# A chunked recurrence whose products are split into a part without the state and a part with it

## The chip, the cores and the metric

One core of one Trainium2 chip runs the whole program. The metric is device time in microseconds (us). The kernel before takes 5064.52 us, the median of three runs (5061.65 to 5067.53).

## The reference

The program is three transformer-like blocks, one after the other, on 1024 tokens of 1024 features in float32. The change lies in the third. That block projects its input, runs a latent attention of 4 heads (`mla_attention`) and beside it a recurrence over tokens for 8 heads of 64 channels, and joins both with a gate and an output projection. The recurrence keeps a 64x64 state S per head:

```python
def step(S, inp):
    r_t, w_t, k_t, v_t, kk_t, a_t = inp
    sa = jnp.einsum('bhvk,bhk->bhv', S, -kk_t)
    S = (S * w_t[:, :, None, :] + sa[..., None] * (kk_t * a_t)[:, :, None, :]
         + v_t[..., None] * k_t[:, :, None, :])
    return S, jnp.einsum('bhvk,bhk->bhv', S, r_t)

xs = tuple(jnp.moveaxis(t.astype(jnp.float32), 1, 0) for t in (r, w, k, v, kk, a))
_, ys = lax.scan(step, jnp.zeros((B, H, N, N), jnp.float32), xs)
```

The outputs `ys` are normalised per head, a bonus term is added, and the result is gated and projected.

## The kernel before

Everything is held with features on partitions, x as `xT`, a tile of 128 partitions by 8 by 1024 that stays in SBUF through the whole program. Work is cut into phases. A phase allocates tiles and semaphores, gives each engine its instructions in a fixed, unrolled order written by hand, and ends when all are done; the next begins then. All transfers named below but a few go over the queue of SyncE (SP); ScalarE (ACT) issues some stores. A queue is worked in order, and so is each engine.

The recurrence is computed in 16 chunks (`NCH`) of 64 tokens (`N = CHUNK`). The 8 heads lie as 4 pairs (`NP`), a pair on 128 partitions; a "block" tile holds a pair as two 64x64 blocks on the diagonal of 128x128, so that one product does both heads. From the decays, `recurrence_inputs_phase` makes four arrays of 512 x 1024: alpha (the key of the past, kk, scaled), beta, kappa and rho (the receptance r, scaled), and stores each row block of 128 to DRAM over ScalarE's queue (L3564). `recurrence_phase` ("wkv" in the trace) then does, per chunk:

- scores of beta against alpha and rho (L3756, eight passes for four pairs), a mask on VectorE (L3825) that gives the system N, stored to DRAM (L3661), and a masked copy for later over ScalarE and GpSimd (L3853, L3729);
- scores of kappa against alpha and rho, copied by ScalarE (L3858) and masked by GpSimd (L3734, L3738). These run beside the back substitution.

After the 16th system is stored, all are loaded back at once, twice 2 MB, with one of the 128 (chunk, head) systems per partition (L3704), and VectorE inverts them by back substitution: 62 steps of an outer product (L3835) and an addition (L3838), each waiting for the one before. The inverse is stored (L3710) and read back as blocks (L3687). Then comes the loop over chunks, in which every product waits for the state or for loads made after the output of the chunk before last (L3653, L3657): beta, kappa and v are transposed on TensorE (L3779) and copied by ScalarE (L3866); the right side w is kappa's mask times v plus alpha times the state; u is the inverse times -w (L3841 copies it); the growth is kappa times v plus beta times u; VectorE adds the state (L3843) and scales by the chunk's decay `ends` (L3845); the output y is three products in one bank, copied (L3879) and stored (L3881). All products of the loop are in float32 and have line L3747.

Ahead of it, `latent_attend_phase` ("mla") puts its 16 output stores (L827) on SyncE's queue behind the loads of all four heads (L816 to L822); VectorE copies outputs to two tiles in turn (L983) and waits for the store before last. Behind it, `last_phase` loads weights and the two halves of the tokens (L3935, L3940, L3947, L3952), multiplies, and adds x, which it transposes from `xT` (L4035).

Of the kernel before, what the change touches and what calls it, by code (L numbers as in the profile page):

```python
# [14 lines left out]
P = 128  # L15
# [754 lines left out]
def latent_attend_phase(nc, name, ident, causal, n_heads, q_rows, qr_rows, k_rows, kr_rows, v_rows, out_rows, scale):  # L770
# [15 lines left out]
    with Phase(nc, name) as ph:  # L786
# [20 lines left out]
        stored = [ph.sem(f"stored{b}") for b in range(2)]  # L807
        block = ph.block()

        @block.sync  # L810
        def _(sp):
# [19 lines left out]
            for hd in range(n_heads):  # L831
                load(hd)
            for m in range(NU // 2):
                store(m)
            for b in range(2):
                sp.wait_ge(stored[b], 16 * (NU // 4))

# [2641 lines left out]
def recurrence_inputs_phase(nc, name, block_ones, ps_rows, kk, decay_sig, rate, k_a, r_k, ends, bonus, out):  # L3479
# [6 lines left out]
    with Phase(nc, name) as ph:  # L3486
# [5 lines left out]
        outs = [ph.sb(f"out{n}", [P, T]) for n in range(4)]  # L3492
# [19 lines left out]
        def _(dve):  # L3512
# [12 lines left out]
            for c in range(RC):  # L3525
# [13 lines left out]
                if c:  # L3539
                    dve.wait_ge(stored, 64 * c)  # L3540
                link(tt(outs[0][:, :], p_prev[:, :], kk[:, c, :], ALU.mult))
                link(tt(outs[1][:, :], rate[:, c, :], kk[:, c, :], ALU.mult))
                link(tt(outs[1][:, :], outs[1][:, :], p_inv[:, :], ALU.mult))
                link(tt(outs[2][:, :], kf[:, :], p_inv[:, :], ALU.mult))
                link(tt(outs[3][:, :], p_now[:, :], r[s][:, :], ALU.mult))
# [9 lines left out]
        def _(act):  # L3555
            for c in range(RC):
# [6 lines left out]
                for n in range(4):  # L3563
                    act.dma_start(out[n][c * P:(c + 1) * P, :], outs[n][:, :]).then_inc(stored, 16)  # L3564
            act.wait_ge(stored, 64 * RC)
# [22 lines left out]
def recurrence_phase(nc, name, ident, masks_dram, ends, alpha_d, beta_d, kappa_d, rho_d, v_d, y_dram, system_d, inverse_d):  # L3588

# [7 lines left out]
    BANKS = 4  # L3603
    with Phase(nc, name) as ph:
        masks = ph.sb("masks", [P, 2, P])
        moving = [ph.sb(f"alpha_rho{s}", [P, NP, 2, N]) for s in range(2)]
        be_sb, ka_sb, v_sb, al_sb = ([ph.sb(f"{n}{s}", [P, NP, P]) for s in range(2)] for n in ("be", "ka", "v", "al"))
        bt_all, rk_all = ph.sb("bt_all", [P, NCH, NP, P]), ph.sb("rk_all", [P, NCH, NP, N])
        rb_all = ph.sb("rb_all", [P, NCH, NP, N])
        n_sb = [ph.sb(f"n{s}", [P, NP, N]) for s in range(2)]  # L3610
        rb_raw, kr_raw = ([ph.sb(f"rb_raw{s}", [P, NP, N]) for s in range(2)], [ph.sb(f"kr_raw{s}", [P, NP, 2, N]) for s in range(2)])
        shared = ph.sb("shared", [P, 2 * N * N + 1024])
        system = shared[:, 0:N * N].rearrange("p (j i) -> p j i", i=N)
        inverse_flat = shared[:, N * N:2 * N * N]
        inverse = inverse_flat.rearrange("p (j i) -> p j i", i=N)
        outer = shared[:, 2 * N * N:]
        part = lambda n: shared[:, n * NP * P:(n + 1) * NP * P].rearrange("p (q n) -> p q n", n=P)
        xt_sb = [part(s) for s in range(2)]
        beta_tok, kappa_tok, v_tok = ([part(2 + 2 * n + s) for s in range(2)] for n in range(3))
        w_sb, u_sb, state, grown = (ph.sb(n, [P, NP, P]) for n in ("w", "u", "state", "grown"))  # L3620
        y_sb = [ph.sb(f"y{s}", [P, NP, N]) for s in range(2)]
        score_ps = [ph.ps(f"score{b}", [P, NP, 2, N]) for b in range(BANKS)]
        tok_ps = [ph.ps(f"tok{b}", [P, NP, P]) for b in range(2)]
# [25 lines left out]
        def _(sp):  # L3649
# [41 lines left out]
            for c in range(NCH):  # L3691
                if c >= 2:
                    sp.wait_ge(n_scored, c - 1)
# [842 lines left out]
```

## Time and profile before

| | |
|---|---|
| median of three runs | 5064.52 us |
| profiled execution | 5060.78 us |
| its span | 5059.0 us |
| TensorE matmul busy | 4028.3 us, 80% |
| VectorE busy | 2727.6 us, 54% |
| ScalarE busy | 1889.4 us, 37% |
| GpSimd busy | 584.0 us, 12% |
| mean granted TensorE clock | 0.88 |

The shares are over the whole program, and the recurrence is a small part of it near the end, so they tell little of it; the timeline of a stretch and its windows tell more. Times in the rows are counted from the start of the span. A window row gives the engines in the order PE (matmuls), PEld (weight loads), DVE (VectorE), ACT (ScalarE), POOL (GpSimd); a Q behind a name marks an issue on that engine's queue. The profiled execution's own time is 1.8 us longer than its span. A matmul's duration holds its way through the array, so durations of neighbours overlap; the distance between starts is what a series costs.

### The profile page before, as it was taken

The numbers are of one execution on the slowest core, as the hardware profiler recorded it, in microseconds if no ns is written. First come the engines' busy times: TensorE is split into PE (matmuls) and PEld (weight loads), VectorE is DVE, ScalarE is ACT, GpSimd is POOL, SyncE is SP. The second block draws the span as 40 slices with busy tenths as digits, with TensorE's granted clock in tenths as the row PEclk, the third lists the DMA queues.
The fourth block names the chain that finished last, engine by engine and source line by source line (L and its number), as shares of the span: only waits on it lengthen the run. The fifth ranks groups of instructions, "written<-read, shape, count | busy, mean of one in ns | idle before, by whom it ended". The sixth has DMA issues, their size and how long they took to land. (4 is left out here: it accounts for less than half of the span.)

```text
span 5059.0 us, 52016 instructions
## 1 busy us (share of the span) xinstructions
PE 4028.3 (80%) x18538; PEld 3132.4 (62%) x18538; DVE 2727.6 (54%) x3066; ACT 1889.4 (37%) x2528; POOL 584.0 (12%) x433
## 2 busy tenths in 40 slices
PE   7996758859995995978669999999969947332679
PEld 5874536248883772845558888888847836122567
DVE  4125754141115776734369999999962235447332
ACT  2114532031113663221237777777741124210123
POOL 1000021042000211012100100101004000013010
PEclk9997878979997997988769999999979978655889
DMA  3222121612222004142159999999932233453351
GB/s 98 96 87 77 41 84 52 208 50 95 100 79 87 26 12 174 56 178 67 67 211 399 383 385 390 386 383 382 383 133 91 89 104 94 158 156 100 82 144 47
DMA packets 488408, 788.24 MB, mean 156 GB/s; under 512 B 172623, under 2 KB 312143, under 8 KB 487112
## 3 DMA queue, kind: packets, MB, share of 16 engines
q1 hardware_dynamic: 453672, 691.46, 39.4%
q10 hardware_dynamic: 29984, 78.13, 4.0%
q0 software_dynamic: 4608, 16.78, 1.3%
q8 instruction: 84, 1.38, 0.1%
q14 instruction: 60, 0.49, 0.0%
HBM read 662.15 MB, written 120.59 MB: 155 GB/s over the span
## 5 line engine op out<-in xcount | busy, mean ns | idle before, releaser
L71 PE MATMUL b_in_acc<-b_in_acts_hi,b_in_w_hi 128*128 128x512 f32 (+1 forms) x1456 | 580.0, 398 | 49.4 <-POOL b_in_acts_lo L749 20.6
L72 PE MATMUL b_in_acc<-b_in_acts_lo,b_in_w_hi 128*128 128x512 f32 (+1 forms) x1456 | 573.2, 394 | 0.0
L73 PE MATMUL b_in_acc<-b_in_acts_hi,b_in_w_lo 128*128 128x512 f32 (+1 forms) x1456 | 573.1, 394 | 0.0
L3184 DVE TENSOR_TENSOR experts_w_lo<-top_xT,experts_w_hi 128x2048 fp32r<-128x2048 f32 x192 | 437.5, 2290 | 62.6 <-ACT experts_w_hi L3129 62.6
L3184 DVE TENSOR_TENSOR experts_w_lo<-experts_ring,experts_w_hi 128x2048 fp32r<-128x2048 f32 x192 | 435.9, 2288 | 32.4 <-ACT experts_w_hi L3129 32.4
L66 DVE CAST b_in_w_hi<-b_in_w 128x1024 fp32r<-128x1024 f32 (+1 forms) x91 | 68.0, 750 | 702.0 <-PE b_in_acc L73 702.0
L3129 ACT ACTIVATE experts_w_hi<-top_xT 128x2048 fp32r<-128x2048 f32 x192 | 367.6, 1919 | 127.1 <-PE experts_gate L73 75.4
L559 ACT ACTIVATE b_in_out<-b_in_acc 128x512 f32<-128x512 f32 (+1 forms) x182 | 109.0, 599 | 810.7 <-PE b_in_acc L73 808.7
L3129 ACT ACTIVATE experts_w_hi<-experts_ring 128x2048 fp32r<-128x2048 f32 x192 | 367.8, 1920 | 116.2 <-PE experts_up L73 66.4
L71 PEld LDWEIGHTS b_in_acc<-b_in_acts_hi,b_in_w_hi 128*128 128x128 f32 (+1 forms) x1456 | 275.4, 189 | 130.1 <-POOL b_in_acts_lo L749 34.9
L73 PEld LDWEIGHTS b_in_acc<-b_in_acts_hi,b_in_w_lo 128*128 128x128 f32 (+1 forms) x1456 | 276.5, 190 | 59.6
L72 PEld LDWEIGHTS b_in_acc<-b_in_acts_lo,b_in_w_hi 128*128 128x128 f32 (+1 forms) x1456 | 276.6, 190 | 56.8 <-issue 0.7
L71 PE MATMUL experts_gate<-experts_w_hi,experts_xg_hi 128*128 128x512 f32 x512 | 201.5, 394 | 4.8 <-DVE experts_w_lo L3184 4.8
L71 PE MATMUL experts_y_ps<-experts_w_hi,experts_act_hi 128*128 128x512 f32 x512 | 205.3, 401 | 0.0
L71 PE MATMUL experts_up<-experts_w_hi,experts_xg_hi 128*128 128x512 f32 x512 | 201.7, 394 | 3.1 <-DVE experts_w_lo L3184 3.1
L73 PE MATMUL experts_y_ps<-experts_w_hi,experts_act_lo 128*128 128x512 f32 x512 | 200.3, 391 | 0.0
L73 PE MATMUL experts_up<-experts_w_hi,experts_xg_lo 128*128 128x512 f32 x512 | 200.1, 391 | 0.0
L72 PE MATMUL experts_gate<-experts_w_lo,experts_xg_hi 128*128 128x512 f32 x512 | 200.1, 391 | 0.0
L73 PE MATMUL experts_gate<-experts_w_hi,experts_xg_lo 128*128 128x512 f32 x512 | 200.0, 391 | 0.0
L72 PE MATMUL experts_up<-experts_w_lo,experts_xg_hi 128*128 128x512 f32 x512 | 199.8, 390 | 0.0
L72 PE MATMUL experts_y_ps<-experts_w_lo,experts_act_hi 128*128 128x512 f32 x512 | 199.6, 390 | 0.0
L2601 PE MATMUL merge_acc<-merge_acts,merge_w 128*128 128x512 f32 x256 | 112.6, 603 | 23.1 <-DMA merge_gate<-proj 23.1
(656 smaller groups left out, 8647.9 us busy)
## 6 DMA issues: line engine op xcount, KB each, us to landing
experts_ring<-in_w_gate SPq DMA_DIRECT2D x128, 1024.0 KB, 7.4
top_xT<-in_w_up SPq DMA_DIRECT2D x128, 1024.0 KB, 9.7
experts_ring<-in_w_down SPq DMA_DIRECT2D x64, 1024.0 KB, 9.5
top_xT<-in_w_down SPq DMA_DIRECT2D x64, 1024.0 KB, 9.3
b_in_w<-in_w_in SPq DMA_DIRECT2D x90, 512.0 KB, 3.8
proj<-b_in_out ACTq DMA_DIRECT2D x90, 512.0 KB, 2.7
mod_w<-in_w_mod SPq DMA_DIRECT2D x12, 2048.0 KB
merge_gate<-proj SPq DMA_DIRECT2D x24, 512.0 KB, 5.9
```

Of the source, the lines that this page charges most:

```text
L66: return nc.vector.tensor_copy(hi, x)
L71: nc.tensor.matmul(out, w_hi, x_hi, start=start, stop=False)
L72: nc.tensor.matmul(out, w_hi, x_lo, start=False, stop=False)
L73: return nc.tensor.matmul(out, w_lo, x_hi, start=False, stop=stop)
L559: nc.scalar.activation(out, acc[s][h][0:m, :], ACT.Sigmoid if gated else ACT.Copy).then_inc(ready, 1)
L2601: mm = nc.tensor.matmul(acc[b][h][:, :], w_sb[s][:, c, :], acts[:, c, h * HALF:(h + 1) * HALF], start=(c == c0), stop=(c == c1 - 1))
L3129: nc.scalar.activation(w_hi[n % HIS][:, :, :], ring[n % RING], ACT.Copy).then_inc(hi_ready, 1)
L3184: nc.vector.tensor_tensor(w_lo[n % HIS][:, :, :], ring[n % RING], w_hi[n % HIS][:, :, :].bitcast(F32), ALU.subtract).then_inc(lo_ready, 1)
```

## The change

`recurrence_phase` becomes two phases, front and back, and alpha and rho no longer go through DRAM.

- The inputs phase writes alpha and rho to a tile `al_rho` that stays on chip, and stores beta and kappa alone.
- The front makes the scores from `al_rho` and four block buffers of beta, with the transposes of beta beside them. ScalarE takes the diagonal blocks of a transposed pair in two copies of 64 partitions. VectorE does all masks; GpSimd only zeroes tiles. While VectorE does the back substitution, with one chunk's masks after every third step, TensorE transposes kappa, v and alpha and makes W = (masked kappa scores) x v and G, Y = v x (kappa, masked rho scores): all that has no state in it. The results are kept for all chunks in `br_all`, `wa_all` and `gy_all`. The inverse is stored in four parts, three of them before its last step.
- The back multiplies, per chunk and pair, the inverse by (W, alpha) at once ("solve"), the alpha part of that by (beta, rho scores) ("transition"), to which VectorE adds the identity and rho; the W part by the same ("at zero"); and the state by the transition ("advance"), in the same bank as "at zero". So one product per pair with the state gives the next state and the output. VectorE adds G and writes the new state twice side by side, TensorE transposes it, and VectorE scales it into blocks.
- `wa_all` lies in `xT`. So the latent attention first stores x to DRAM (4 MB) and the last phase loads it again.

Its core:

```diff
             for hd in range(n_heads):
                 load(hd)
+            sp.dma_start(x_spill, xT[:, :, :]).then_inc(x_spilled, 16)
             for m in range(NU // 2):
                 store(m)
...
-                link(tt(outs[0][:, :], p_prev[:, :], kk[:, c, :], ALU.mult))
+                link(tt(al_rho[:, c, 0, :], p_prev[:, :], kk[:, c, :], ALU.mult))
...
-                for n in range(4):
+                for n in range(2):
                     act.dma_start(out[n][c * P:(c + 1) * P, :], outs[n][:, :]).then_inc(stored, 16)
...
+def recurrence_front_phase(...):                      # SyncE
+            sp.wait_ge(zeroed, 4)
+            for c in range(4):
+                load_beta(c)
...
             for c in range(NCH):
+                store_system(c)
+                if c + 4 < NCH:
+                    load_beta(c + 4)
+                if c == 11:
+                    for x in range(4):
+                        load_second(x)
+            for s in range(4):
+                sp.wait_ge(n_stored[s], 16 * (NCH // 4))
+            for dst in (system, inverse):
+                sp.dma_start(dst[:, :, :], system_d.rearrange("(p j) i -> p j i", j=N)).then_inc(system_loaded, 16)
+            for x in range(4, 3 * NCH):
+                load_second(x)
+                if x == 30:
+                    store_inverse(48, 64)
+            store_inverse(32, 48)
+            store_inverse(16, 32)
+            store_inverse(0, 16)
...
+            def second(c):                             # TensorE
+                for x in range(3 * c, 3 * c + 3):
+                    pe.wait_ge(bd_loaded[x % 4], 32 * (x // 4 + 1))
+                    if x == 3 * c:
+                        score(NCH + c, bd[x % 4], c)
+                    turn(NCH + x, bd[x % 4])
...
             for c in range(NCH):
+                pe.wait_ge(be_loaded[c % 4], 32 * (c // 4 + 1))
+                score(c, be_bd[c % 4], c)
+                turn(c, be_bd[c % 4])
+            second(0)
+            for c in range(NCH):
+                if c + 1 < NCH:
+                    second(c + 1)
+                products(c)
...
+            def mask_keys(c):                          # VectorE
+                dve.wait_ge(scored, NCH + c + 1)
+                if c >= 2:
+                    dve.wait_ge(gy_ready, c - 1)
...
+            for c in range(FIRST_MASKS):
+                mask_keys(c)
             dve.wait_ge(system_loaded, 32)
...
                 tt(inverse[:, 0:k, k + 1:N], inverse[:, 0:k, k + 1:N], prod, ALU.add).then_inc(row_added, 1)
+                c = FIRST_MASKS + n // SPACING         # both 3
+                if n % SPACING == SPACING - 1 and c < NCH:
+                    mask_keys(c)
...
+def recurrence_back_phase(...):                        # TensorE
+            solve(0)
+            solve(1)
+            transition(0)
+            at_zero(0)
+            solve(2)
+            transition(1)
+            for c in range(NCH):
+                advance(c)                             # waits moved 2c+2, state_ready c+1
+                if c + 3 < NCH:
+                    solve(c + 3)                       # waits ux_copied c+2
+                if c + 1 < NCH:
+                    at_zero(c + 1)                     # waits y_copied c
+                    turn(c)                            # waits summed c+1
+                if c + 2 < NCH:
+                    transition(c + 2)                  # waits ux_copied c+3, moved 2c+2
...
+            for c in range(NCH):                       # VectorE
+                if c + 1 < NCH:
+                    add_state(c)
+                add_output(c)
+                if c + 1 < NCH:
+                    next_state(c)
+                if c + 2 < NCH:
+                    evict_transition(c + 2)
...
+            sp.dma_start(xT[:, :, :], x_spill).then_inc(x_loaded, 16)   # last_phase, before load_mix(1, c)
```

In the back, ScalarE's two copies of u for chunk c wait until `advance(c - 2)` is done; each of the loads of the inverse is made four chunks ahead.

## Rows read from the trace of the kernel before

**Rows 1.** Timeline at the recurrence's bounds: start us, us, engine, line, operation.
```profile
4483.36 0.45 ACTq L3564 DMA_DIRECT2D rw_beta<-rw_in_out  x1
...
4490.70 0.99 POOL L3724 MEMSET wkv_be<- 128x512 f32 x2 [397.14 <-POOLq L39]
...
4889.65 1.76 SPq L3935 DMA_DIRECT2D last_mix<-rw_wkv  x4
```

**Rows 2.** Timeline, one chunk of the first scores.
```profile
4510.49 2.05 PE L3756 MATMUL wkv_score<-wkv_alpha_rho,wkv_be 128*128 128x128 f32 x8 [0.85 <-DMA wkv_alpha_rho<-rw_rho]
...
4510.53 1.24 SPq L3653 DMA_DIRECT2D wkv_be<-rw_beta  x2
...
4512.57 0.42 DVE L3825 TENSOR_TENSOR wkv_n<-wkv_score,wkv_masks 128x256 f32<-128x256 f32 x1 [2.48 <-PE wkv_score L3756]
```

**Rows 3.** Timeline, the system's way back on chip.
```profile
4563.44 0.92 SPq L3704 DMA_DIRECT2D wkv_shared<-rw_system  x2
...
4577.82 0.11 DVE L3828 MEMSET wkv_shared<- 128x64 f32 x1 [19.83 <-DMA wkv_shared<-rw_system]
...
4579.10 3.11 PE L3756 MATMUL wkv_score<-wkv_alpha_rho,wkv_ka 128*128 128x128 f32 x13 [11.73 <-DMA wkv_ka<-rw_kappa]
```

**Rows 4.** Timeline of VectorE in the back substitution.
```profile
4652.51 1.19 DVE L3835 TENSOR_TENSOR wkv_shared<-wkv_shared 128x992 f32<-128x992 f32 x1
...
4671.78 1.12 DVE L3835 TENSOR_TENSOR wkv_shared<-wkv_shared 128x920 f32<-128x920 f32 x1
...
4707.63 0.22 DVE L3838 TENSOR_TENSOR wkv_shared<-wkv_shared 128x62 f32<-128x62 f32 x1
```

**Rows 5.** Windows: stretch, us, each engine's busy us, PEclk, DMA share, GB/s.
```profile
4226.00:4246.00 20.00, 19.77 (x121) 17.70 (x120) 11.79 (x25) 12.77 (x27) 0.00 (x0) 1.00 0.16 47
...
4510.00:4530.00 20.00, 10.30 (x41) 9.01 (x41) 2.22 (x6) 2.31 (x6) 4.34 (x6) 0.50 0.61 138
...
4578.00:4624.00 46.00, 28.07 (x115) 24.73 (x116) 44.66 (x40) 8.37 (x14) 38.98 (x26) 0.54 0.51 115
...
4712.00:4716.00 4.00, 4.00 (x25) 4.00 (x24) 0.00 (x0) 0.61 (x2) 0.00 (x0) 0.63 0.35 139
...
4724.00:4780.00 56.00, 48.33 (x403) 44.93 (x402) 10.81 (x16) 14.71 (x27) 0.00 (x0) 1.00 0.44 99
```

**Rows 6.** Timeline of the loop over chunks.
```profile
4723.75 0.69 DVE L3845 TENSOR_TENSOR wkv_state<-wkv_grown,b3c_ends 128x512 f32<-128x512 f32 x1
...
4770.02 0.65 PE L3779 MATMUL wkv_tok<-top_squares,wkv_be 128*128 128x128 f32 x4 [0.60 <-DMA wkv_be<-rw_beta]
...
4770.77 0.60 ACT L3866 ACTIVATE wkv_shared<-wkv_tok 128x512 f32<-128x512 f32 x1 [1.61 <-PE wkv_tok L3779]
...
4776.22 0.97 PEld L3747 LDWEIGHTS wkv_y_ps<-wkv_rb_all,wkv_u 128*128 128x128 f32 x8
...
4777.11 0.97 PEld L3747 LDWEIGHTS wkv_score<-wkv_shared,wkv_bt_all 128*128 128x128 f32 x8
...
4886.69 0.69 DVE L3845 TENSOR_TENSOR wkv_state<-wkv_grown,b3c_ends 128x512 f32<-128x512 f32 x1
```

**Rows 7.** DMA issues: KB each, median us from issue to landing.
```profile
rw_beta<-rw_in_out ACTq DMA_DIRECT2D x4, 512.0 KB, 3.8
...
wkv_be<-rw_beta SPq DMA_DIRECT2D x64, 64.0 KB, 2.3
...
x_spill<-top_xT SPq DMA_DIRECT2D x2, 4096.0 KB, 16.3
```

**Rows 8.** Timeline of the latent attention, stores and third copy-out.
```profile
4226.51 12.22 SPq L827 DMA_DIRECT2D mixed<-mla_out  x3
...
4237.96 0.42 DVE L983 COPY mla_out<-mla_o 128x256 f32<-128x256 f32 x1
```

**Rows 9.** Timeline of the last phase.
```profile
4922.06 0.58 SPq L3940 DMA_DIRECT2D last_mix<-mixed  x1
...
4954.64 1.10 PE L3992 MATMUL last_turned<-last_mix,top_squares 128*128 128x512 f32 x2
```

More of the change, by code:

```diff
@@ L3612, in recurrence_phase @@
[L3612 to L3623, printed above, removed]
-        u_ps, y_ps = ph.ps("u_ps", [P, NP, P]), ph.ps("y_ps", [P, NP, N])
-        w_ps, grown_ps = (score_ps[b][:, :, :, :].rearrange("p q o n -> p q (o n)") for b in range(2))
-        masks_loaded, zeroed, xt_zeroed = ph.sem("masks_loaded"), ph.sem("zeroed"), ph.sem("xt_zeroed")
@@ L3739, in _, with score @@
-            pool.wait_ge(row_added, STEPS)
-            for s in range(2):
-                nc.gpsimd.memset(xt_sb[s], 0.0).then_inc(xt_zeroed, 1)
+            for tile in be_bd + [t[:, :, :] for t in bd]:
+                nc.gpsimd.memset(tile, 0.0).then_inc(zeroed, 1)
         @block.tensor
         def _(pe):
-            def product(out, lhsT, rhs, start, stop):
+            def score(x, keys, c):
+                if x >= 3:
+                    pe.wait_ge(masked, x - 2)
+                bank = score_ps[x % 3]
@@ new lines, in products @@
+            def products(c):
+                s = c % 2
+                pe.wait_ge(tok_copied, turn_no(c, 1) + 1)
+                pe.wait_ge(bt_ready, c + 1)
+                if c:
+                    pe.wait_ge(w_copied, c)
+                for q in range(NP):
+                    mm = nc.tensor.matmul(w_ps[:, q, :], bt[s][:, q, :], v_tok[s][:, q, :], start=True, stop=True)
+                mm.then_inc(w_ready, 1)
+                pe.wait_ge(masked, NCH + c + 1)
+                if c:
+                    pe.wait_ge(gy_copied, c)
+                for q in range(NP):
+                    mm = nc.tensor.matmul(gy_ps[:, q], v_tok[s][:, q, :], kr[s][:, q], start=True, stop=True)
+                mm.then_inc(gy_ready, 1)
@@ L3882, in _ @@
-            for s in range(2):
-                act.wait_ge(y_stored[s], 16 * (NCH // 2))
-def last_phase(nc, name, ident, ones, block_ones, mix_rows, wkv_rows, gate_rows, bonus, ln_g, ln_b, w_dram, post_g, xT, out_dram):
+                    act.wait_ge(sy_ready, c - 1)
+                src = ux_ps[c % 2][:, :, :, :].rearrange("p q a n -> p (q a) n")
+                for h in range(2):
+                    r = slice(64 * h, 64 * h + 64)
+                    copy = nc.scalar.activation(ux_bd[c % 2][r, :, r], src[r, :, :], ACT.Copy)
```

458 lines of the change are left out of this document (248 added, 210 removed).

## The prediction

> **What bounds the kernel now.** I read the busy shares first: they say only that TensorE leads over all stages together, and the change touches one stage. So I went to the stage's timeline for its three parts, then to the windows for the clock in each, and last to the stages before and behind it that the spill of x touches.
>
> The recurrence runs from the first memset at 4490.70 to the next phase's first load at 4889.65, 399 us [rows 1]. Part one, scores of all 16 chunks until the system is back on chip, ends at 4577.82 [rows 3]: 87.1 us. Per chunk there are eight TensorE passes (2.05 us) and a VectorE mask (0.42 us), but the queue issues two beta loads (1.24 us) and two more of alpha and rho before each, and TensorE waits for them ([rows 2]: "<-DMA wkv_alpha_rho<-rw_rho"). Part two is 62 pairs of VectorE operations, one after the other, 4577.82 to 4707.85: 130.0 us [rows 3, 4]. Its second half takes 4707.85 - 4652.51 = 55.3 us and the first 74.7, with the same sizes in reverse order; in the first GpSimd is busy 39 of 46 us [rows 5]. Part three is the loop over chunks: the state is ready at 4723.75 and for the last time at 4886.69 [rows 6], fifteen periods of 10.86 us. Each goes round y, the next chunk's loads (1.24 us of issue, 2.3 to land), the transposes, the right side, u, the state. TensorE is granted the full clock there (1.00, 2.4 GHz) at 86% busy, and half of it (1.2 GHz) in part one [rows 5].
>
> **The change part by part.** Unit costs. Four fp32 products of a 128-column pair: groups start 0.89 us apart at the full clock [rows 6], so 1.78 at half (the 2.05 of [rows 2] has the tail in it). Four transposes: 0.65 with the tail [rows 6], 0.43 in a row of work; 0.85 at half. VectorE from PSUM, 128x512: 0.69; 128x256: 0.42. ScalarE 128x512: 0.60; the diagonal copies are two of these over 64 partitions, and since partitions run side by side I take each at the full tile's time (ux: 2 x 0.60 = 1.2). No row shows half-tile copies or operands broadcast from PSUM; the bounds are 0.42 and 1.19 (a 992-element SBUF operation, [rows 4]), and 0.69 is nearest in size.
>
> *A, the inputs phase.* Two stores per row block instead of four. The second of the four is issued at 4483.36 and such a second one lands after 3.8 us: 4487.2, where now the next phase starts at 4490.70 [rows 1, 7]. **-3.5** (0 to -5.5, with the waits between row blocks).
>
> *B, until back substitution starts.* Four memsets before the first load instead of eight: 2.0 us. Load 1.2 + 2.3 [rows 2, 7]: first score at 5.5. Then per chunk: TensorE score + transposes, 2.65 us at half clock, 1.33 at full; queue 1.24 + 0.4 and gaps = 1.7; VectorE 0.84; ScalarE 0.8. TensorE starts at half clock and has no gap, and in [rows 5] the clock rose within 4712 to 4716, with TensorE busy all of it (0.63 there, 1.00 later). So two chunks at 2.65 and 14 at 1.7 (the queue's): 29.1. The eight extra loads placed at chunk 11 hold the last stores by 1.2 (5.1 us of issue less the loads that no longer follow). Mask and store 0.9, landing 2.3, then both system loads, 14.4 from issue to use as now [rows 3]. That is 53.4. But now something is late next: VectorE must make mask_keys(0..2) first, and the third needs score(18), which TensorE's queue has behind two transposes and products(0). Their operands' loads are issued after the 4 MB of the system, on the same queue; today the same loads are used at 4579.10, 1.3 after the system [rows 3]. So 1.3 + 2 x 0.85 + 3.56 + 1.78 + tail 0.25 at half clock + the two masks 1.15 = 9.8. Sum 63.1 against 4577.82 - 4490.70 = 87.1: **-24.0**.
>
> *C, back substitution.* GpSimd's masks are gone from beside it: 2 x 55.3 = 110.7. Added in the same queue: 13 mask_keys of 0.69 + 0.42 + gap = 1.15: 15.0. VectorE can wait for TensorE: a chunk there is 36 passes' worth, 4.0 us full (3 x 0.89 for one score and two products, 3 x 0.43 for the transposes), 8.0 half; six loads are 3.8 us of queue; ScalarE's six half and two whole copies 3.4. VectorE's three pairs plus mask grow from 3 us (operations of 0.22 at size 62) to 8.3 (1.19 at size 992, [rows 4]), so only the first two or three masks come before their scores: I take 3 us of waits in all. With the diagonal's memset 128.8 against 130.0: **-1.2** (-4 if nothing waits; all at half clock below).
>
> *D, store, load, loop.* Only the last quarter of the inverse is stored behind the last row: 0.5 MB, 3.8 as the store of that size in [rows 7], and 0.4 for the phase's end. Then memset 0.5, load 3.5, solve at half clock 2.05, copy 1.2, and transition, two adds (0.84), at_zero, solve, transition in part beside each other: first advance ends 13.3 after the phase began. The period: TensorE's order is advance, solve, at_zero, turn, transition. Turn starts 3 x 0.89 = 2.67 after advance began; its sum on VectorE (1.11 + 0.69 and hand-offs = 2.0) is ready before, so the work that is free of the state hides it. Turn ends 0.65 later, next_state 0.69, hand-offs 0.19: next advance at 4.20, transition (to 4.0) hidden. VectorE has 2.64 in it, ScalarE 1.2, the queue 1.7. 15 x 4.2 = 63.0. Last output 0.4, store 0.4 + 2.3, phase change 0.3. Sum 83.9 against 4889.65 - 4707.85 = 181.8 [rows 1, 4]: **-97.9**.
>
> *E, the spill.* It is issued before the first output store of the latent attention, and 4 MB took 16.3 us [rows 7]. The first store, issued at 4226.51 and now landing at once, would land near 4226.5 + 16.3 = 4243; the third copy-out (4237.96) waits for it [rows 8], 5 us, with VectorE's maxima queued behind and TensorE, 99% busy [rows 5], behind those with two units in hand. **+4** (0 to +8).
>
> *F, x back.* 4 MB ahead of the second half's inputs, issued now at 4922.06; they come near 4940 and the first use is at 4954.64 [rows 9]. 0 (at most +3).
>
> Sum -122.6: the profiled 5060.8 (span 5059.0) becomes 4938, and as the median of runs lies 3.7 above it, **4942**.
>
> One rule speaks against B and C. The windows [rows 5] show TensorE at 0.54 of the clock while it is 61% busy in short groups, and at 1.00 in the loop, where 12 of 76 passes a chunk are transposes. The Trainium skill, TensorE: Matmul & The Clock Gate, Part 4: PE-mode transpose, says that the full clock does not engage for transposes, which do not count as busy in the same way. By that rule the front, a third of whose passes are transposes, would stay at half clock; the row of the loop shows only that one in six does no harm.
>
> **The rivals.**
> Front at half clock, 0.2: TensorE's transposes or its pauses between chunks keep it at 1.2 GHz. B: 16 x 2.65 - 29.1 = +13.3. C: score(31) comes -1.2 + 13 x 8.0 = 102.8 after the start, then a mask 1.15 and the last 23 pairs, 4707.85 - 4671.78 = 36.1 [rows 4]: 140.1, +11.4. 4942 + 25 = 4967. For it: the 0.54; against: today's groups are 2 us of work between waits, the new ones longer.
> Loop at half clock, 0.08: 4 x 1.78 + 0.85 = 8.0 per period, +57 and +4 at its head: 5003. Against: 86% busy kept 1.00, and the new loop is fuller.
> The products are not made beside the substitution, 0.06 (the change does not do what it says): the two in-order queues wait on each other and 13 chunks of 4.0 come on top: +52, 4994.
> Slower, 0.04: the loop's look-ahead fails, because ux_copied, moved and sy_ready close one ring, and every step waits for the last at half clock: four groups of 2.05, transposes 1.09, adds 0.69 + 0.69 + 0.84, copy 1.2, six hand-offs 0.9 = 13.6 a period, 15 x 9.4 = +141: 5083. It decides from 4.2 + 122.6/15 = 12.4 us. Against: banks and tiles are doubled, and no wait I find asks for the same iteration.
>
> **How the numbers follow.** The forecast has 0.62; its own bounds (A, E, F, the waits of C, half-tile operations) make it 4920 to 4962. From the rivals the range takes the front's and most of the 4994: 4915 to 4995, about 0.85. A measurement can tell 0.2% (10 us) from no change. Only the last case is slower: 0.04; between them next to nothing, 0.01; faster 0.95.
>
> **What would show it.** The last phase's first load near 4767 (4889.65 now); a period of 4.2 between state writes; the clock 1.0 there; no GpSimd operation beside back substitution and no pair above 1.2 us; a start of it some 10 us behind the system's landing; one idle of 4 to 6 us on VectorE in the latent attention near its third copy-out. It is wrong if the period is over 6 us, or if the substitution lasts over 140.

## The result, and the profile after

The changed kernel takes 4929.32 us (median of four runs, 4922.44 to 4939.38), the kernel before 5063.09 us beside it: a ratio of 0.9739, 95% interval 0.9717 to 0.9761, or 133.8 us less. The forecast was 4942, 122.6 less, with a range of 4915 to 4995. Run once more later, the changed kernel gave 0.9738 (0.9720 to 0.9757). The profiled execution took 4933.41 us, its span is 4931.6 us.

I read the new trace by the same stretches as the old one. The bounds first (timeline of the changed kernel: start us, us, engine, line, operation); they answer to [rows 1]:

```profile
4491.52 0.45 ACTq L3567 DMA_DIRECT2D rw_kappa<-rw_in_out  x1
...
4496.39 1.92 POOL L3693 MEMSET b3a_gy_all<- 128x512 f32 x4 [395.79 <-POOLq L39]
...
4764.36 1.76 SPq L4050 DMA_DIRECT2D last_mix<-rw_wkv  x4
```

The recurrence lasts 268 us instead of 399. One scoring chunk, beside [rows 2]: TensorE's eight passes take 1.16 us instead of 2.05, and the beta loads are all it waits for:

```profile
4521.34 1.16 PE L3702 MATMUL wkv_front_score<-b3a_al_rho,b3a_gy_all 128*128 128x128 f32 x8 [0.28 <-DMA b3a_gy_all<-rw_beta]
4521.67 1.06 SPq L3647 DMA_DIRECT2D rw_system<-b3a_gy_all  x1
4522.34 0.60 PE L3709 MATMUL wkv_front_tok<-top_squares,b3a_gy_all 128*128 128x128 f32 x4
4522.78 1.23 SPq L3638 DMA_DIRECT2D b3a_gy_all<-rw_beta  x2
```

The way back of the system, beside [rows 3]. VectorE's last wait in front of the substitution ends with a score, not with the transfer. The system's second 2 MB had landed at 4552.84, 8.1 us before the diagonal's memset. TensorE had to wait for the v of chunk 1, which was issued behind the system, and did the four groups of work up to that score at half clock (granted 0.50 from 4553 to 4559):

```profile
4539.30 0.33 SPq L3680 DMA_DIRECT2D wkv_front_system<-rw_system  x1
...
4553.40 1.97 PE L3709 MATMUL wkv_front_tok<-top_squares,wkv_front_bd 128*128 128x128 f32 x8 [15.01 <-DMA wkv_front_bd<-shifted]
...
4559.92 0.69 DVE L3794 TENSOR_TENSOR wkv_front_bt<-wkv_front_score,wkv_front_masks 128x512 f32<-128x512 f32 x1 [20.91 <-PE wkv_front_score L3702]
4560.53 0.41 DVE L3796 TENSOR_TENSOR wkv_front_kr<-wkv_front_score,wkv_front_masks 128x256 f32<-128x256 f32 x1
4560.95 0.11 DVE L3808 MEMSET wkv_front_inverse<- 128x64 f32 x1
```

Inside the substitution, beside [rows 4], two masks stand between the end of one sum (4584.80) and the start of the next product (4585.65), 0.85 us, and the last row ends at 4683.84:

```profile
4583.89 0.91 DVE L3818 TENSOR_TENSOR wkv_front_inverse<-wkv_front_inverse,wkv_front_outer 128x720 f32<-128x720 f32 x1
4584.72 0.68 DVE L3794 TENSOR_TENSOR wkv_front_bt<-wkv_front_score,wkv_front_masks 128x512 f32<-128x512 f32 x1
4585.32 0.41 DVE L3796 TENSOR_TENSOR wkv_front_kr<-wkv_front_score,wkv_front_masks 128x256 f32<-128x256 f32 x1
4585.65 0.93 DVE L3815 TENSOR_TENSOR wkv_front_outer<-wkv_front_system,wkv_front_inverse 128x752 f32<-128x752 f32 x1
...
4683.62 0.22 DVE L3818 TENSOR_TENSOR wkv_front_inverse<-wkv_front_inverse,wkv_front_outer 128x62 f32<-128x62 f32 x1
```

The windows (columns as in [rows 5]: the busy us of TensorE, its weight loads, VectorE, ScalarE, GpSimd, then the granted clock): 1.00 in the first loop of the front, 0.94 and 0.91 beside the substitution, 1.00 in the loop over chunks, where TensorE is busy 58.46 of 62 us. GpSimd does nothing.

```profile
4506.00:4532.00 26.00, 20.50 (x159) 17.65 (x158) 11.11 (x30) 10.41 (x28) 0.00 (x0) 1.00 0.55 125
4572.00:4600.00 28.00, 24.27 (x197) 23.13 (x196) 27.28 (x37) 19.01 (x46) 0.00 (x0) 0.94 0.42 101
4600.00:4640.00 40.00, 24.10 (x182) 23.05 (x181) 39.14 (x41) 16.72 (x40) 0.00 (x0) 0.91 0.23 56
4702.00:4764.00 62.00, 58.46 (x494) 55.90 (x492) 35.45 (x72) 15.37 (x26) 0.00 (x0) 1.00 0.25 56
```

One period of the loop, beside [rows 6]. TensorE goes from advance to advance in 4.23 us. VectorE has finished the sum (at 4712.89) long before the turn at 4713.79, and then waits 1.20 us for the turn. TensorE's five groups, at the distances at which they follow each other without a wait, come to 4 x 0.89 + 0.43 = 3.99 us. A part of the other 0.24 is a wait: the second advance starts 1.04 us after the transition, and 0.15 after VectorE has written the state (4715.12):

```profile
4711.04 1.13 PE L3908 MATMUL wkv_back_sy_ps<-wkv_back_move,wkv_back_state 128*128 128x128 f32 x8
4712.00 1.06 PE L3886 MATMUL wkv_back_ux_ps<-top_xT,wkv_back_xt 128*128 128x128 f32 x8
4712.90 1.06 PE L3901 MATMUL wkv_back_sy_ps<-b3a_br_all,wkv_back_ux 128*128 128x128 f32 x8
4713.79 0.60 PE L3915 MATMUL wkv_back_turned<-top_squares,wkv_back_twice 128*128 128x128 f32 x4
4714.23 1.06 PE L3894 MATMUL wkv_back_mr_ps<-b3a_br_all,wkv_back_ux 128*128 128x128 f32 x8
4715.27 1.13 PE L3908 MATMUL wkv_back_sy_ps<-wkv_back_move,wkv_back_state 128*128 128x128 f32 x8
```
```profile
4712.20 0.69 DVE L3962 TENSOR_TENSOR wkv_back_twice<-wkv_back_sy_ps,b3a_gy_all 128x512 f32<-128x512 f32 x1 [0.35 <-PE wkv_back_sy_ps L3908]
4712.81 0.41 DVE L3969 TENSOR_TENSOR wkv_back_y<-wkv_back_sy_ps,b3a_gy_all 128x256 f32<-128x256 f32 x1
4714.43 0.69 DVE L3973 TENSOR_TENSOR wkv_back_state<-wkv_back_turned,wkv_back_ends_bd 128x512 f32<-128x512 f32 x1 [1.20 <-PE wkv_back_turned L3915]
```

The price of the spill, beside [rows 8]: the third copy-out waits for an output store that stands behind the 4 MB, and the sixteen stores spread over 91.33 us instead of 87.83 (87.83 is the whole group of which [rows 8] shows the first three). The wait goes on to TensorE, which is idle for 3.03 us. Behind that its granted clock is 0.50 for a while (the last row is a window, with the clock third from its end), and from the fourth copy-out to the fifth it is 1.4 us longer than before.

```profile
4233.59 0.43 SPq L834 DMA_DIRECT2D x_spill<-top_xT  x1
4234.07 91.33 SPq L828 DMA_DIRECT2D mixed<-mla_out  x16
...
4247.74 0.42 DVE L986 COPY mla_out<-mla_o 128x256 f32<-128x256 f32 x1 [2.62 <-DMA mixed<-mla_out]
...
4255.89 1.09 PE L873 MATMUL mla_turned<-top_squares,mla_probs 128*128 128x128 f32 x4 [3.03 <-DVE mla_probs L980]
...
4256.00:4258.00 2.00, 2.00 (x9) 1.82 (x9) 1.56 (x4) 0.99 (x2) 0.00 (x0) 0.50 0.20 66
```

In the last phase the load of x is issued at 4797.45, and VectorE then waits 6.82 us for gate rows that stand behind it (beside [rows 9]):

```profile
4797.45 0.58 SPq L4086 DMA_DIRECT2D top_xT<-x_spill  x1
4812.40 0.69 DVE L4294 TENSOR_TENSOR last_mix<-last_mix,last_gate 128x512 f32<-128x512 f32 x1 [6.82 <-DMA last_gate<-proj]
```

While VectorE waits there, GpSimd makes four tiles of weights, and does it in 11.44 us instead of 13.20; TensorE, which stands behind them by way of ScalarE, waits 3.49 us instead of 5.10. The kernel before, then the changed one:

```profile
4928.45 13.20 POOL L4265 TENSOR_TENSOR last_w_lo<-last_out,last_w_hi 128x1024 fp32r<-128x1024 f32 x4 [6.83 <-DVE last_w_hi L66]
4942.91 1.86 PE L4022 MATMUL last_col<-top_squares,last_square 128*128 128x1 f32 x8 [5.10 <-ACT last_square L4106]
...
4803.85 11.44 POOL L4382 TENSOR_TENSOR last_w_lo<-last_out,last_w_hi 128x1024 fp32r<-128x1024 f32 x4 [6.84 <-DVE last_w_hi L66]
4816.55 1.87 PE L4138 MATMUL last_col<-top_squares,last_square 128*128 128x1 f32 x8 [3.49 <-ACT last_square L4223]
```

By step, in the two profiled executions (before, after, difference, forecast):

| step | before | after | difference | forecast |
|---|---|---|---|---|
| A, first exponential of the inputs phase to the recurrence | 67.21 | 63.11 | -4.1 | -3.5 |
| B, first memset to the diagonal's memset | 87.12 | 64.56 | -22.6 | -24.0 |
| C, from there to the last row's end | 130.03 | 122.89 | -7.1 | -1.2 |
| D, from there to the last phase's first load | 181.80 | 80.52 | -101.3 | -97.9 |
| E, first to last output store of the latent attention | 87.83 | 91.33 | +3.5 | +4 |
| F, last phase | 169.35 | 167.24 | -2.1 | 0 |

The sum is -133.7 against a forecast of -122.6. The spans differ by 127.4; the 6.3 between the two figures are in stretches that the change doesn't touch (the latent attention starts at 4195.56 instead of 4188.14; over all traces below it starts anywhere from 4186 to 4198).

### The profile page after: what moved, and what is told of

It reads as the page before. It is cut to its first block and busy times, and to the rows that moved or that the text cites. A ratio compares the mean times of both kernels' runs of the same rounds, so it can differ in the third digit from the quotient of the medians.

```text
span 4931.6 us, 51740 instructions
## 1 busy us (share of the span) xinstructions
PE 3980.8 (81%) x18406; PEld 3092.5 (63%) x18406; DVE 2736.7 (55%) x3152; ACT 1912.6 (39%) x2608; POOL 526.0 (11%) x385
## 5 line engine op out<-in xcount | busy, mean ns | idle before, releaser
L71 PE MATMUL b_in_acc<-b_in_acts_hi,b_in_w_hi 128*128 128x512 f32 (+1 forms) x1456 | 579.1, 398 | 52.3 <-POOL b_in_acts_lo L749 22.6
```

The costliest lines, as they stand in the source:

```text
L71: nc.tensor.matmul(out, w_hi, x_hi, start=start, stop=False)
```

## Experiments

Such shifts make single medians blunt for effects of 3 to 8 us, so the small edits are read by the same stretches of their traces. In twelve traces of the changed kernel and its variants a stretch that the edit doesn't touch varies by 1.6 us for A, 1.9 for B, 1.1 for D, 0.3 for C, and 3.1 for E. B and C together are 185.9 to 187.5 us where neither is edited. But for experiments 7 and 11, each is one execution.

**1. The kernel before, once more**

> The kernel before once more, for a second execution of its stretches, since every comparison by stretch rests on one. If the stretches are the kernel's own and only their start moves: first to last output store of the latent attention 87.8 within 0.1; from the first exponential of the inputs phase to the recurrence 67.2 within 0.7; back substitution 130.0 within 0.5; from its last row to the last phase 181.8 within 0.5; last phase 163 to 170, as it spreads in the changed kernel. If instead a stretch is off by over 1.5 us, the step that it prices is open by as much.

5065.8 us; another execution of the same kernel on that chip took 5081.94. Stores 87.90, A 66.31, B 86.34, C 129.96, D 184.41, last phase 168.48. C and E repeat within 0.1. A is 0.9 lower and D is 2.6 higher, beyond what I expected: the old loop waits for transfers in every period, and the size of D is open by about that much, -101 to -104. The steps' sum over both executions of before and all fitting ones of the changed kernel (A -4.1, B -22.4, C -7.2, D -102.6, E +3.9, F -2.8) is -135.2, where the medians differ by 133.8.

**2. The spill on GpSimd's own queue** (step E)

```diff
-            sp.dma_start(x_spill, xT[:, :, :]).then_inc(x_spilled, 16)
+        def _(pool):
+            pool.wait_ge(o_copied, 1)
+            nc.gpsimd.dma_start(x_spill, xT[:, :, :]).then_inc(x_spilled, 16)
```

> The changed kernel with the spill of x (4 MB) issued by GpSimd's own DMA queue, at the first copy-out, instead of ahead of the output stores on SyncE's. Read on the stretch from the first load of the latent attention to the first load of the recurrence's inputs phase: 131.7 us in the changed kernel, 128.1 in the one before. Theory Q (the stores stand behind the spill in one queue, in order): the 2.62 us wait of the third copy-out goes and the stretch is 128 to 128.5. Rival B (the 4 MB take the transfer engines from the stores whichever queue they come by): the wait stays at 2 us or more and the stretch stays within 131 to 132.5.

4927.15 us. The sixteen stores go out within 87.82 us, the figure of the kernel before to a hundredth, and no copy-out waits for a store. The stretch that I had named, which ends at the first load of the phase right behind the latent attention, fell to 125.0, lower than the 128.1 of before and than theory Q's 128 to 128.5; it holds the varying loads at the phase's start, so the stores are the better measure. Timeline of this kernel:

```profile
4231.04 0.63 POOL L843 DMA_DIRECT2D x_spill<-top_xT  x1 [130.45 <-DVE mla_out L990]
4231.18 87.82 SPq L828 DMA_DIRECT2D mixed<-mla_out  x16
```

Theory Q holds in its result: with the spill off SyncE's queue the step costs nothing. It does not follow that the 4 MB are free for the stores beside them, and that part of rival B stands. GpSimd issued the spill at 4231.04, and its bytes moved from 4234.5 to 4245.2. The first store, issued at 4231.18, landed at 4235.41, well ahead of the third copy-out, which needs it. The second, issued at 4237.47 into the midst of the 4 MB, landed 8.4 us after its issue, against 1.8 in the kernel before. That cost nothing because the copy-out which needs it came at 4250.61.

With the spill in front of them the stores took 89.97 to 93.05 us in ten traces, 91.8 on average: the step is worth +3.9. The ten traces also tell why it varies. The idle time of TensorE behind the late copy-out is 2.9 to 3.4 us in each. In three of them the granted clock stays at 1.00 behind it, and the stores take 90.0 to 90.1. In the other seven it is at half for a while, 0.62 to 0.77 on average from the fourth copy-out to the fifth; these two are then 6.7 to 8.2 us apart instead of 5.4, and the stores take 91.3 to 93.1. So the wait costs 2.2 us and the clock behind it up to 2.8 more. What decides between the two cases no run here shows.

**3. Two masks ahead of the substitution** (B against C)

```diff
-    FIRST_MASKS, SPACING = 3, 3
+    FIRST_MASKS, SPACING = 2, 3
```

> The changed kernel with two kappa masks ahead of the back substitution instead of three (the other 14 inside it, one after every third pair). Theory M (the start waits for the third mask, whose score has the v of chunk 1 behind the 4 MB of the system on the queue): the diagonal's memset comes at the landing of the system, 57 to 59 us after the first memset of the front instead of 64.6; the third mask, after three pairs, then waits 0 to 3 us, so the last row comes 3 to 6 us earlier than now. Rival S (the system's own landing sets the start, and the mask only looks late): the start stays at 63 to 65.

4925.7 us. B 57.38, C 127.0, together 184.4 (187.5 before the edit): -3.1. Timeline of VectorE: the start now waits for the transfer, and the third mask, three pairs later, for its score.

```profile
4551.40 0.11 DVE L3808 MEMSET wkv_front_inverse<- 128x64 f32 x1 [14.06 <-DMA wkv_front_inverse<-rw_system]
...
4558.03 0.69 DVE L3794 TENSOR_TENSOR wkv_front_bt<-wkv_front_score,wkv_front_masks 128x512 f32<-128x512 f32 x1 [4.53 <-PE wkv_front_score L3702]
```

Theory M holds: 7.2 us of the changed kernel's start were the third mask's wait (its own trace has 8.1 from the landing to the start). But most of it only moved: the wait inside, put at 0 to 3 us, is 4.5. Against the spread of the unedited sums, 185.9 to 187.5, the gain is 1.5 to 3.1 us.

**4. Three tiles ahead of the system on the queue**

```diff
+            for x in range(4, 7):
+                load_second(x)
             for s in range(4):
                 sp.wait_ge(n_stored[s], 16 * (NCH // 4))
```

> The changed kernel with the next three tiles of the second part (v and alpha of chunk 1, kappa of chunk 2... six loads, 1.9 us of issue) issued ahead of the system's two loads instead of behind them. Theory M: the third mask is ready before the system lands; the system is issued 0 to 3 us later, since these loads wait for the transposes of the tiles they replace; the start of the back substitution is 58 to 62 us after the first memset (64.6 now), with no wait for a score in front of it. Rival S: start 65 to 67, later by what the system is issued later.

4919.23 us. B 60.78 as theory M has it, but a wait of 4.63 us for the fourth mask's score appears inside, C is 126.3, and the sum 187.1 is unchanged. I had missed that: whichever tile is the first behind the 4 MB, its chunk is late, and with a mask after every third pair it stops VectorE.

**5. The masks later in the substitution**

```diff
-                c = FIRST_MASKS + n // SPACING
-                if n % SPACING == SPACING - 1 and c < NCH:
+                c = FIRST_MASKS + (n + 1 - FIRST_PAIR) // SPACING
+                if n + 1 >= FIRST_PAIR and (n + 1 - FIRST_PAIR) % SPACING == 0 and c < NCH:
```

with two masks ahead and FIRST_PAIR = 8.

> The changed kernel with two kappa masks ahead of the back substitution, and the other 14 inside it after pairs 8, 11, 14, ... instead of 3, 6, 9, ... Theory M2 (the start is set by the landing of the system, and the wait of 4.5 us that appeared inside with two masks is only the third score, which the loads behind the system deliver later): start 57 to 58 us after the first memset, no wait above 0.3 us inside, substitution 121 to 122.5: together 179 against 187.5 now and 184.4 with two masks. Rival C (the chunks of the second part themselves are too slow for one mask in three pairs this early): waits of 1 to 3 us reappear at the later masks and the sum stays at 182 to 185.

4924.47 us. B 56.27, C 122.21, no wait inside: 178.5, 9.0 less than the changed kernel's 187.5 and 7.4 less than the lowest unedited sum. M2 holds, C falls. Where the masks stood was a choice of the change that cost it 7 to 9 us.

**6. The system loaded once and copied on chip**

```diff
-            for dst in (system, inverse):
+            for dst in (system,):
...
+            nc.scalar.activation(inverse[:, N // 2:N, :], system[:, N // 2:N, :], ACT.Copy).then_inc(inv_copied, 1)
...
+            nc.vector.tensor_copy(inverse[:, 0:N // 2, :], system[:, 0:N // 2, :]).then_inc(inv_copied, 1)
...
```

> As the kernel with late masks, and the system is loaded once (2 MB) instead of twice; the second tile is copied from the first on chip, half by VectorE and half by ScalarE. Theory D (the transfer engines' rate sets the landing: 14.4 us from issue to use for 4 MB): 7.5 to 9 us from issue to landing, copy 1.5 to 2.5; the start comes 51 to 54 us after the first memset and no wait follows: start and substitution together 173 to 176. Rival F (a fixed part of the landing dominates, because the two loads run beside each other on all engines): landing 11 us or more, start 56 or later.

4920.19 us. B 53.70, C 122.26: 176.0. Timeline of this kernel:

```profile
4542.53 0.33 SPq L3680 DMA_DIRECT2D wkv_front_system<-rw_system  x1
...
4551.01 1.23 DVE L3810 COPY wkv_front_inverse<-wkv_front_system 128x2048 f32<-128x2048 f32 x1 [8.57 <-DMA wkv_front_system<-rw_system]
4553.05 0.11 DVE L3812 MEMSET wkv_front_inverse<- 128x64 f32 x1 [0.81 <-ACT wkv_front_inverse L3779]
```

2 MB land 8.5 us after issue and the copy takes 2.0, as theory D has it; 4 MB took 13.9 in experiment 3. So the landing is not all rate: the second 2 MB add 5.4 us, and 3.1 of the 8.5 come whatever the size (an estimate from these two figures).

**7. GpSimd at work beside the substitution** (step C)

```diff
+            pool.wait_ge(diag_ready, 1)
+            for n in range(28):
+                w = (P, N)[n % 2]
...
+                nc.gpsimd.tensor_tensor(be_bd[3][:, :, 0:w], be_bd[2][:, :, 0:w], be_bd[2][:, :, 0:w], ALU.mult).then_inc(idled, 1)
...
```

> The changed kernel with 28 GpSimd products of its own on the chip's SBUF beside the back substitution, 14 of 128x512 and 14 of 128x256, as many and as large as the kernel before had there (their results are used by nobody). Theory P (GpSimd and VectorE hold each other up): the substitution grows from 122.9 us by 15 to 25 while GpSimd is busy, and the median by about 20, to a ratio of 0.977 to 0.979. Rival L (the first half was slow before because of the loads that landed beside it, or of its own shapes): it stays within 122 to 125 and the ratio at 0.974.

Ratio 0.9749 (0.9733 to 0.9766), against 0.9739: the two can't be told apart, and theory P's 0.977 to 0.979 was too high. The trace is sharper: C is 133.2, +10.3 (the waits of 1.3 us inside are gone, since VectorE is later), and L falls. Of P the cause holds and the size does not: it is less than 15 because these products, without broadcast operands, were shorter than those of before: busy 29.3 us (groups of this kernel: count, busy us, mean ns) instead of 43.6 in the old first half (14 of each size, 24.9 and 18.7).

```profile
L3699 POOL TENSOR_TENSOR b3a_gy_all<-b3a_gy_all 128x512 f32<-128x512 f32 x14 | 17.3, 1234 | 62.3 <-DVE wkv_front_inverse L3816 61.3
L3699 POOL TENSOR_TENSOR b3a_gy_all<-b3a_gy_all 128x256 f32<-128x256 f32 x14 | 12.0, 859 | 1.1
L3823 DVE TENSOR_TENSOR wkv_front_outer<-wkv_front_system,wkv_front_inverse 128x62 f32<-128x62 f32 (+30 forms) x62 | 59.5, 960 | 1.7
L3826 DVE TENSOR_TENSOR wkv_front_inverse<-wkv_front_inverse,wkv_front_outer 128x62 f32<-128x62 f32 (+30 forms) x62 | 58.7, 947 | 2.1
```

The 124 products and sums of VectorE come to 118.2 us instead of 106.5 (53.2 + 53.3): 11.7 us for 29.3 of GpSimd, 0.40 per us. In the kernel before it was 19.4 for 43.6, 0.44. The same pair of 440 elements takes 1.34 and 0.91 us beside GpSimd, 0.62 and 0.62 without.

**8. The loop with the turn ahead of the state-free products** (step D)

```diff
                 advance(c)
+                if c + 1 < NCH:
+                    turn(c)
                 if c + 3 < NCH:
                     solve(c + 3)
                 if c + 1 < NCH:
                     at_zero(c + 1)
-                    turn(c)
```

> The changed kernel with the loop's TensorE order changed alone: advance, turn, solve, at_zero, transition, so that the turn waits for VectorE's sum with nothing of the other chunks before it. Theory T (in the changed kernel TensorE's own work sets the period, and solve and at_zero fill the time of the sum): the sum and its hand-offs, 2.0 us less what next_state now hides, come on top; the period goes from 4.23 to 5.5 to 6.2 us, the phase up by 18 to 28 us. Rival V (VectorE or the ring of the state sets the period and TensorE only waits in it): the period stays within 4.0 to 4.4.

4930.4 us. The period is 5.01, D is 90.7, +10.1. V falls; T has the sign but not the size. TensorE of this kernel:

```profile
4701.28 1.06 PE L3908 MATMUL wkv_back_sy_ps<-wkv_back_move,wkv_back_state 128*128 128x128 f32 x8
4703.12 0.66 PE L3915 MATMUL wkv_back_turned<-top_squares,wkv_back_twice 128*128 128x128 f32 x4 [0.79 <-DVE wkv_back_twice L3963]
```

From advance to turn it is 1.84 us, not 2.9: the sum that the turn needs is one VectorE operation of 0.69 (state, with the PSUM operand read twice), not 1.11 + 0.69.

**9. The loop without at_zero**

```diff
             def advance(c):
+                if c >= 2:
+                    pe.wait_ge(y_copied, c - 1)
...
-                    mm = nc.tensor.matmul(sy_ps[c % 2][:, q], state_bd[c % 2][:, q, :], move[c % 2][:, q], start=False, stop=True,
+                    mm = nc.tensor.matmul(sy_ps[c % 2][:, q], state_bd[c % 2][:, q, :], move[c % 2][:, q], start=(q == 0), stop=True,
...
-            at_zero(0)
...
                 if c + 1 < NCH:
-                    at_zero(c + 1)
                     turn(c)
```

With `at_zero` gone, `advance` is the first to write the bank, so it opens it and takes over the wait for the output's sum.

> The changed kernel without the four products per chunk of at_zero (left out: the state-free part of state and output, so the values of y are others). Theory T (TensorE's work sets the period): 0.89 us less of it in each period, 4.23 to 3.35 or, if the ring of the state is next, to 3.43 as in the last three periods, which have no solve; the phase 11 to 13 us shorter. Rival V (VectorE or the ring sets the period): it stays at 4.0 to 4.3.

4918.74 us. The period is 3.44, and D 69.4, 11.1 less. T holds, with the ring of the state next (the round from advance over the sum, the turn and the new state to the next advance): 0.89 us less of TensorE's work took 0.79 off the period, the turn now starts 0.06 us after the sum, and VectorE waits only 0.42 for each turn.

```profile
4703.36 0.69 DVE L3973 TENSOR_TENSOR wkv_back_state<-wkv_back_turned,wkv_back_ends_bd 128x512 f32<-128x512 f32 x1 [0.42 <-PE wkv_back_turned L3917]
4706.80 0.69 DVE L3973 TENSOR_TENSOR wkv_back_state<-wkv_back_turned,wkv_back_ends_bd 128x512 f32<-128x512 f32 x1 [0.42 <-PE wkv_back_turned L3917]
```

**10. Three times the transposes in the first loop** (the clock)

```diff
-                for q in range(NP):
+                for q in list(range(NP)) * (3 if x < NCH else 1):
```

> The changed kernel with each transpose of the first loop of the front issued three times (same operands, same place), so that 12 of 20 TensorE passes of a chunk there are transposes instead of 4 of 12. Theory W (transposes keep the full clock as products do): the granted clock in the first loop rises to 1.00 as now, a chunk costs TensorE 0.89 + 3 x 0.43 = 2.2 us instead of the queue's 1.93, and the first loop gets 3 to 6 us longer. Rival X (the full clock is not given where transposes are the larger part): granted clock 0.5 to 0.6 through the loop, 2 x 2.2 = 4.3 us a chunk, the loop 35 us longer.

4922.14 us. Chunks follow each other every 2.20 us, and from the first chunk's scores to the last's it is 35.8 us instead of 30.1, +5.7; B is 66.8, only 2.3 above the changed kernel's 64.6. The windows of TensorE in this kernel, the second one inside the loop (stretch, us, busy us, clock):

```profile
4488.76:4494.76 6.00, 5.04 (x23) 0.50 0.41 98
4494.76:4520.76 26.00, 26.00 (x236) 0.99 0.52 117
```

W holds and X falls: with 12 of 20 passes transposes the clock is 0.99. A stretch of transposes alone was not run.

**11. The three edits together, and the changed kernel beside it**

> The changed kernel with what the single edits gave put together: spill of x by GpSimd's queue, two kappa masks ahead of the back substitution and the others after pairs 8, 11, ..., one load of the system and a copy on chip. If the parts add, as their places apart in the program let expect: -4.0 (output stores of the latent attention 87.8 instead of 91.9 us) and -11.5 (front to last row 176 instead of 187.5): 15 us under the changed kernel on the same chip, ratio to the kernel before 0.971 where the changed kernel has 0.974. Rival (the spill beside other transfers, or the earlier loads, give it back elsewhere): under 8 us.

> The changed kernel once more, as the neighbour on the same chip of the kernel with all three edits. Ratio to the kernel before 0.972 to 0.976; stretches of the trace within 0.5 us of those seen: first memset to start of the back substitution 63 to 65, substitution 122.5 to 123, from there to the last phase 80 to 81; first to last output store of the latent attention 90 to 93.

All three: ratio 0.9691 (0.9674 to 0.9707); the changed kernel on the same chip 0.9738 (0.9720 to 0.9757). The median of all three is 4914.75 us; one of its six runs took 7540.94 at a granted clock of 0.73 (0.89 in the others), has no trace to explain it and is outside the ratio. By trace the spans are 4911.2 and 4926.1: stores 87.84 and 92.82, B + C 176.4 and 187.1, D 79.9 and 80.7. The parts add: 16.5 us by stretch and 14.9 by span, where I had said 15; the two ratios are 0.0047 apart, 24 us, with intervals that allow 7 to 42. It has the lowest median of all kernels here.

## Why the prediction was right, and where it was off

The mechanisms were right: fewer transfers, GpSimd out of the way, a loop whose state-free work hides the sum. The forecast was 12.7 us above the median, and that it was not further off is in part luck: B and E came out near by two errors each that cancel.

**A** was right in kind, 0.6 short. The last block's second store landed 4.5 us after its issue, not 3.8, which is the median of all four blocks. From the last block's first store to the next phase it is 5.2 us instead of 7.7, -2.5 for the -3.5 forecast; the earlier blocks' waits, which I had left to the bound, gave 1.6 (blocks are 15.6 us apart, 16.3 and 16.9 before).

**B** was right in its causes. The loads of alpha and rho and the half clock are gone, a chunk takes 1.9 to 2.0 us. The term for the stage was 1.4 us too good, and that is a difference of two. The system landed 56.5 us after the first memset, not 53.4: the eight extra loads placed at chunk 11 hold the last four systems' stores longer than the 1.2 us that I gave them, and the last of these was issued 40.5 us after the memset where the working has 36.7. "Something is late next", the third mask behind the 4 MB, held as told, half clock included, but took 8.1 us from the landing instead of 9.8 (experiment 3, without the third mask, started 7.2 earlier).

**The clock.** The first loop's granted clock of 1.00 (2.4 GHz) with a third of the passes transposes, and of 0.99 with 60%, leaves nothing of the rival "front at half clock", 4967, but for the first 3 us of TensorE's work in the front (0.50 from 4500 to 4504) and the 6 us behind TensorE's wait of 15. The rule of the Trainium skill (TensorE: Matmul & The Clock Gate, Part 4: PE-mode transpose), that the full clock does not engage for transposes, is not borne out by either trace: fp32 transposes between fp32 products kept the clock that the products had. For transposes alone no run here tells.

**C** is the step whose size failed, -7.1 for -1.2. Its mechanism held: GpSimd out of the way, 2 x 55.3 for the pairs. Two additions were too dear. Two masks were priced at 1.15 us with a gap; they overlap, and with 2 x 55.3 for the pairs, 1.3 of waits and 0.15 for the diagonal, 122.9 leaves (122.9 - 112.0) / 13 = 0.84 for them: 13 x 0.31 = 4.0. The waits were put at 3 us, and are 0.83 + 0.43 = 1.3: 1.7. Together 5.7 of the 5.9.

**D** was right: period 4.23 for 4.2, clock 1.00. The way through it is the one forecast: TensorE's work from advance to turn (2.75 us for 2.67), then turn, new state and hand-offs (1.48 for 1.53), with the transition hidden beside these. Experiments 8 and 9 show that the first part is work of TensorE and not the wait for the sum. The forecast was 3.4 us too dear in four places: the last store and the change of phase took 3.1 us instead of 4.2; the first advance ended 12.6 after the phase's start instead of 13.3; the fifteen periods sum to 61.8 instead of 63.0, since the last two, without a solve, are 3.4; the tail was 0.3 less. One term was wrong without harm: the sum ahead of the turn was taken as 2.0 us and is 0.95, so the cover of 1.78 us of state-free work was larger than I thought; experiment 8, reasoned from the same term, missed by 0.5 to 1.2 us a period for it.

**E** was right in sum (+3.5 there, +3.9 over ten traces, for +4), and that by luck. The wait was 2.6 us, not 5, since the 4 MB let the store through 14.1 us after the spill's issue, not 16.3; it is worth 2.2 in the stores. The rest, 0 to 2.8, is TensorE's clock behind its idle time of 3 us (experiment 2), of which the forecast had nothing.

**F** was 0 by argument; the last phase is 163.2 to 167.6 us in twelve traces and 168.5 and 169.4 in the two of before. It is shorter though it loads 4 MB more, and the traces tell of some 2 us of that. VectorE's wait for the gate rows costs TensorE nothing; GpSimd, for which TensorE waits at that time, has the chip's SBUF more to itself. Its four operations take 11.0 to 11.4 us in the twelve traces and 13.2 in the two of before (the first of them 4.0 for 5.8), and TensorE's wait behind them is 2.8 to 3.5 us instead of 5.1 and 5.2. It is what experiment 7 shows, seen from GpSimd's side; no run here tests it by itself.

Of the signs named, one was missed: the idle time near the third copy-out, put at 4 to 6 us, was 2.6; and the start some 10 us behind the system's landing was 8.1. The rivals: products not beside the substitution (no: waits of 1.3 us in all), loop at half clock (no: 1.00), a failed look-ahead (no: 4.23 us). The error of the forecast by stretch, 11.1 us, is C with 5.9, D with 3.4, F with 2.1, A with 0.6 and E with 0.5, less 1.4 of B.

## What to carry to other kernels

Here a large transfer held what was issued behind it on its queue until it had landed. What helped: another queue (-3.9 us, though the store that ran beside it there was late too, and only went unneeded), a smaller transfer (2 MB and a 2 us copy instead of 4 MB), and an order in which no engine needs a thing behind it before that can be there. Moving one consumer to the other side of a wait (experiments 3 and 4) bought 0 to 3 us, since the next one stood right behind.

A wait can cost more than it lasts: 3 us without work on TensorE cost up to 2.8 us more by the clock behind it (experiment 2).

In a recurrence, write down which engine's work fills the period and which ring would be next. Here the period was 4.23 us, with 3.99 of TensorE's work in it, and the ring alone 3.44: only the difference, 0.8 us a chunk, could be had by less state-free work.

## What the runs showed of the hardware

GpSimd's elementwise operations on SBUF lengthen VectorE's beside them by 0.40 to 0.44 us for each us that GpSimd is busy, in two kernels with different operands; VectorE's operations from PSUM, the masks, kept their 0.68 and 0.41 us. It goes the other way too: a GpSimd operation of 128x1024 took 5.8 us beside a busy VectorE and 4.0 beside a waiting one (last phase, twelve traces against two).

After 2.9 to 3.4 us without work TensorE's granted clock was at half for a while in seven of ten traces of one place in the latent attention, and stayed at 1.00 in three (experiment 2).

A store issued on SyncE's queue while 4 MB moved by GpSimd's queue landed after 8.4 us instead of 1.8 (experiment 2); behind the same 4 MB on its own queue the first store landed 13.6 us after its issue.

ScalarE's copies of 64 partitions by 512 elements take as long as of 128 (1.19 us for two), and VectorE reads a PSUM operand twice by broadcast at the price of the full size, 0.69 us for 128x512: both as estimated.
